# Adding the last expert sums apart from the stored rows, and a later first weight load, at a layer boundary

## The reference, cut to what matters

```python
# end of layer 0, for context and latent tokens alike
y = jnp.zeros_like(hf)
for e in range(N_EXPERTS):
    a = jax.nn.silu(hf @ w_gate[e]) * (hf @ w_up[e])
    y = y + combine[:, e:e + 1] * (a @ w_down[e])
x = x + g2 * y                        # ctx = ctx + cg2 * y
# start of layer 1
h = _rmsnorm(x, norm1[l]) * (1 + sc1) + sh1
q_a, k_a, v_a, q_b, k_b, v_b, q_n, k_n, v_n, gate_l = jnp.split(h @ w_in[l], IN_OFFSETS, axis=-1)
```

## Time and profile before

| | us |
|---|---|
| median of 3 runs | 1623.99 (1623.52 to 1628.21) |
| profiled execution, its own time | 1625.1 |
| profiled execution, span from first to last instruction | 1623.3 |
| TensorE busy | 1556.6 |
| granted clock, mean share of full | 0.975 |

### The profile page before, as it was taken

One profiled execution on the slowest core, in us unless ns is written; L12 is line 12 of the kernel. 1 busy time (PEld: TensorE's weight loads), 2 busy tenths in 40 slices (PEclk: granted clock), 3 DMA queues, 4 the chain that ended last, 5 costly groups with the idle time before them and its releaser, 6 DMA issues. The chain is left out here.

```text
span 1623.3 us, 16361 instructions
## 1 busy us (share of the span) xinstructions
PE 1556.6 (96%) x6186; PEld 743.0 (46%) x6186; DVE 658.9 (41%) x1409; ACT 340.1 (21%) x784; POOL 131.7 (8%) x212
## 2 busy tenths in 40 slices
PE   8999999999999999899999988999999998989796
PEld 4444456644444444654444434446654444433232
DVE  2232068776677724611111126503766327211113
ACT  3011178810000021101011014114830011100001
POOL 1000001200000010200100020000210010111010
PEclk9999999999999999899999998999999997999898
DMA  9912430135535360699999797543139775999996
GB/s 341 298 54 102 159 133 2 40 106 156 200 139 192 144 233 39 231 347 365 413 407 417 296 374 272 155 168 117 27 123 343 277 281 210 376 411 408 415 374 277
DMA packets 110528, 382.39 MB, mean 236 GB/s; under 512 B 24945, under 2 KB 29185, under 8 KB 93872
## 3 DMA queue, kind: packets, MB, share of 16 engines
q1 hardware_dynamic: 96112, 330.32, 54.6%
q0 software_dynamic: 13904, 50.71, 8.7%
q10 hardware_dynamic: 432, 0.29, 0.1%
HBM read 367.00 MB, written 30.47 MB: 245 GB/s over the span
## 5 line engine op out<-in xcount | busy, mean ns | idle before, releaser
L2180 PE MATMUL bank<-ring_sb,HT_sb 128*128 128x512 f32 x544 | 240.2, 594 | 0.0
L2077 PE MATMUL bank<-ring_sb,HT_sb 128*128 128x512 f32 x384 | 170.0, 598 | 2.5 <-ACT HT_sb L964 2.5
L2180 PEld LDWEIGHTS bank<-ring_sb,HT_sb 128*128 128x128 f32 x544 | 102.4, 190 | 131.8 <-issue 131.8
L1253 DVE SCALAR_TENSOR_TENSOR MB_sb<-ring_sb,cT_sb,MB_sb 128x512 f32<-128x512 f32 x192 | 144.3, 752 | 6.8
L2184 PE MATMUL bank<-ring_sb,QR_sb 128*128 128x512 f32 x288 | 129.5, 592 | 0.0
L2348 PE MATMUL bank<-ring_sb,HT_sb 128*64 128x512 f32 x544 | 123.4, 607 | 0.7 <-ACT HT_sb L1134 0.7
L2077 PEld LDWEIGHTS bank<-ring_sb,HT_sb 128*128 128x128 f32 x384 | 72.2, 192 | 89.3 <-issue 89.3
L2372 PE MATMUL bank<-ring_sb,QR_sb 128*64 128x512 f32 x336 | 82.4, 635 | 17.1 <-DMA ring_sb<-w_e_down 14.5
L2074 PE MATMUL bank<-HT_sb,ring_sb 128*128 128x512 f32 (+1 forms) x256 | 97.4, 539 | 0.0
L1097 ACT ACTIVATE WK_sb<-bank 128x512 f32<-128x512 f32 x36 | 21.5, 597 | 341.2 <-PE bank L2180 341.1
L2184 PEld LDWEIGHTS bank<-ring_sb,QR_sb 128*128 128x128 f32 x288 | 54.7, 190 | 68.9 <-issue 68.9
(11 more groups left out here) (356 smaller groups left out, 1759.0 us busy)
## 6 DMA issues: line engine op xcount, KB each, us to landing
ring_sb<-w_e_down SPq DMA_DIRECT2D x32, 2048.0 KB, 15.4
ring_sb<-w_mod SPq DMA_DIRECT2D x24, 2048.0 KB, 9.3
ring_sb<-w_in SPq DMA_DIRECT2D x21, 2048.0 KB, 17.7
ring_sb<-w_e_gate SPq DMA_DIRECT2D x16, 2048.0 KB, 12.0
ring_sb<-w_e_up SPq DMA_DIRECT2D x16, 2048.0 KB, 13.1
ring_sb<-w_e_gate SPq DMA_DIRECT2D x22, 1024.0 KB, 16.9
ring_sb<-w_e_up SPq DMA_DIRECT2D x22, 1024.0 KB, 18.6
ring_sb<-w_branch SPq DMA_DIRECT2D x8, 1024.0 KB, 12.8
```

The lines of the kernel that those rows point to most:

```text
L1253: link(stt(a, WR[slot][:, k], cT[:, k, strm:strm + 1], a, ALU.mult, ALU.add))
L2077: ins = mm(bank[j % 4][:, :], HT[:, k, P * t:P * t + P], WR[slot][:, k], start=(k == 0), stop=(k == KD - 1))
L2180: ins = mm(bank[i % 2][:, :], HT[:, k, P * t:P * t + P], WR[wg][:, k], start=(k == 0), stop=(k == KD - 1))
```

## The change

Three things. For tiles 0 and 1 first_rows no longer waits for TensorE's last sums and no longer adds them: it only multiplies the rows, over 1024 columns in one instruction, as it does for tiles 2 and 3. The last sums of tiles 0 and 1 are then gated and added by add_last, after add_rows. The scaling of tile 0 stands behind second_rows(1) in place of ahead of it. And SyncE awaits the gathered rows of tile 0 before it issues kvab of layer 1.

```diff
@@ SyncE, the loads of a layer
+                    if key == ("kvab", 1):
+                        eng.wait_ge(ygat_in[0], 32)
                     if key == ("qa", 1):
                         for t in range(NT):
                             eng.wait_ge(ygat_in[t], 32)
@@ VectorE, first_rows
                     y0 = ygat[t][0]
-                    if t < 2:
-                        eng.wait_ge(add_mm, NT * l + t + 1)
-                        for half in range(2):
-                            cols = slice(CW * half, CW * half + CW)
-                            ins = stt(y0[:, cols], y0[:, cols], r_w[:, t, 0:1], add_bank[t][half][:, :], ALU.mult, ALU.add)
-                        link(ins)
-                    else:
-                        link(ts(y0, y0, r_w[:, t, 0:1], None, ALU.mult))
+                    link(ts(y0, y0, r_w[:, t, 0:1], None, ALU.mult))
@@ VectorE, add_rows
                     link(tt(y0, y0, gout[:, t // NLAT], ALU.mult))
-                    ins = tt(X[:, t], X[:, t], y0, ALU.add)
-                    if t < 2:
-                        ins.then_inc(x_moe, 1)
-                        eng.wait_ge(x_moe, NT * l + t + 1)
-                    else:
-                        link(ins)
+                    link(tt(X[:, t], X[:, t], y0, ALU.add))
@@ VectorE, layer 0's end
                     for t in range(NT):
                         first_rows(t)
-                        if t:
+                        if t >= 2:
                             scaled(1, t - 1)
                         second_rows(t)
+                        if t == 1:
+                            scaled(1, 0)
                         add_rows(t)
-                        if t >= 2:
-                            add_last(t)
+                        add_last(t)
                     scaled(1, NT - 1)
```

## The result

| | us |
|---|---|
| kernel before, median of 10 runs beside it | 1625.76 (1622.90 to 1629.77) |
| changed kernel, median of 10 runs | 1630.20 (1626.47 to 1634.58) |
| ratio, 95% interval | 1.0029 (1.0016 to 1.0042) |
| span of the profiled execution | 1628.5 (before 1623.3) |

The change costs 4.7 us (2.6 to 6.8), where 1.5 was forecast, and 1630.2 lies above the range. In these runs the kernel before was itself 1.8 us above the median that the forecast started from, so 1.8 us of the miss is the base and some 3 us the change.

What follows compares the result with a forecast made beforehand. TensorE was taken to bound, the boundary's shift passing through: rows -1.2, order +2.13 and +0.48 give +1.4 us, topped to +1.5 by kvab's weights. Median 1623.99 becomes 1625.5; range 1622.8 to 1628.4.

Steps and rivals of the forecast that it cites:

- VectorE's order: Layer boundary: tile 0's last sums after its rows cost +2.13 us, its scaling behind second_rows(1) +0.48 us.
- what bounds, and that the boundary's shift is passed on: TensorE, busy 96% of the span, bounds; whatever the layer boundary gains or loses arrives at the end unchanged.
- Tile 0 starts at 967.85 - 1.2: Tile 0's first VectorE instruction: with kvab late, the gathered rows land 1.2 us sooner, at 966.65.
- (a): Store of yd ahead of the gathers: lands 0.6 us sooner without kvab's packets beside it, bounds 0 to 1.0.
- (b): Tile 0's gathers: land 0.6 us faster without kvab's last packets beside them, bounds 0 to 1.3.
- kvab goes out at about 966.75 ... I take the middle of these two, 980.6: kvab, issued among the gathers, lands at 980.6, between 980.1 and 981.1, 0.3 us ahead of VectorE's path.
- the upper bound: kvab's latest landing, 981.1: gathers' data from 962.3, 12.6 us for the gathers and 6.2 for kvab.
- the sum holds as long as kvab is the last to finish: Bus at the boundary: gathers' time plus kvab's gives kvab's landing, whatever share of packets each gets.
- The weights become the wait: Rival: kvab served only after the gathers, landing 984.1; TensorE +4.6, with the clock +5.3, whole time 1629.3; chance 0.12.

Runs made afterwards that it cites:

- e1: Changed kernel without SyncE's wait ahead of kvab, so only VectorE's new order, against the kernel before: ratio 1.0017 (1.0008 to 1.0026).
- e7: Kernel before with 20 unused products ahead of the last sums of tiles 0 and 1: ratio 1.0075 (1.0058 to 1.0092).
- e8: e1 with 20 unused products ahead of the last sums of tiles 0 and 1: ratio 1.0076 (1.0059 to 1.0093) against the kernel before.
- e2: Kernel before with only kvab's wait for tile 0's gathered rows added, VectorE's order unchanged: ratio 1.0018 (1.0008 to 1.0028).
- e3: Kernel before with kvab waiting for the gathered rows of all four tiles: one run, 1629.91 us, with 1626.11 for the kernel before beside it.
- e12: Kernel before with kvab waiting only for the stores of yd, as GpSimd does ahead of the gathers: ratio 1.0022 (1.0012 to 1.0033).
- e6: Kernel before with the down weights of layer 0's last expert as four DMAs with 4 KB packets instead of one with 16 KB: ratio 1.0007 (0.9991 to 1.0023).
- e4: Kernel before with only the second of kvab's two 1 MB pieces waiting for tile 0's rows: ratio 1.0000 (0.9989 to 1.0011).
- e11: e6 and e4 together, plus a separate semaphore for tile 0's first gather, against the kernel before: ratio 1.0002 (0.9991 to 1.0013).

## Why the prediction was wrong

**Right: VectorE's order.** Forecast +2.13 and +0.48 from tile 0's start to the scaled tile, +2.61; measured +2.60 in the changed kernel (10.62 to the transposes against 8.02) and +2.69 in e1. e7 and e8 show its reason: with the sums last, the same order gains 2.0 us.

**Right: what bounds, and that the boundary's shift is passed on.** wb0's load went out 4.3 to 5.5 us later, after the first product had come 4.4 to 5.0 later.

**Wrong: "Tile 0 starts at 967.85 - 1.2".** Half of this was to come from the store (a), half from the gathers (b). The store took 11.0 us in the changed kernel and 10.4 in e2, with kvab early 10.4, 11.1 and 10.6: nothing. From first gather to tile 0's start it took 7.05, 7.88 and, in e3, 6.94 us with kvab late, 6.94, 6.90 and 6.94 with it early: nothing. (The 7.88 is not kvab's doing either, which in e2 goes out only then; so a single profile can be off by 0.9 us here.) The early kvab lies in a gap: in the changed kernel, without it, the bus carried a single packet between 956 and 960, and before the change all but kvab's last packets had moved when the gathers' first came, at 962.8. Those last packets, until 964.2, do delay the first gather, which landed 5.1 us after its issue with kvab early and 4.2 or 4.3 in e2 and e3. But tile 0 waits for its second gather, and that took 5.6 in e3 as before. e12 shows what real contention would have been, 3.2 us, and no kernel but that one and e6 had it. The change removed a cost that was not there.

**Wrong, and the step that decided: "kvab goes out at about 966.75 ... I take the middle of these two, 980.6".** That is +14.6 from the last sums; it landed at +18.5. The sum had two terms: the gathers' data start, at -3.7, and from there 18.3 us until all that moves ahead of kvab's last packet has moved. The data started at -2.8, 0.8 us later, since the store gave the gathers nothing. The stretch was 21.3 us, 3.0 longer, and that is the term that was mis-sized. Its rate was right: forecast 6.3 MB in the 18.8 us of the upper bound, 0.335 MB/us; measured 7.0 MB from the gathers' first packet to kvab's last, in 20.7 us, 0.338. Its bytes were not. The prediction says that "the sum holds as long as kvab is the last to finish"; but it put qa's load behind kvab on the queue and left it out of the sum, and qa's packets did not wait for kvab's end. All packets of the changed kernel from 978 to 980.9:

```profile
DMA packets 757, 1.07 MB, mean 369 GB/s; under 512 B 15, under 2 KB 454, under 8 KB 757
```

The 303 that are not under 2 KB are qa's. Their 0.62 MB are 1.8 us at the measured rate; 0.6 us more passed from kvab's last packet to its landing, and 0.5 us is the choice of the middle over the upper bound. This split is worked out from the traces. e4 agrees with it, but no run holds qa back and leaves the rest, so what qa's packets cost is an estimate. What e3 does show is that a landing can't be had as issue time plus a duration here: issued 7.5 us later than in e2, kvab was there at the same moment.

So the first product started at the later of +16.8 (order, rows not sooner) and +18.5 (weights), not at +15. The rival *The weights become the wait* had given +4.6 at TensorE and 1629.3 for the whole; its wait was the case, and I gave it 0.12. That its number is close is in part luck: it had kvab moving only after the gathers and alone, and kvab in fact moved a third of its packets beside them and the rest mixed with qa's. The 14.7 us that kvab was early looked like slack to give away, and the later issue used all of it and 5 us more. The Trainium skill (DMA: Bandwidth & Descriptors, Rules for kernel authors) advises to issue a DMA early and wait late. The trace agrees with the advice; the page's reason is the fixed setup cost, and here it was the other traffic.

**Open.** In e2 the boundary lost 4.4 to 4.9 us and the whole time 2.9 (1.3 to 4.5); in e7 the boundary lost 15.4 to 16.1 and the whole time 12.2 (9.4 to 15.0). The profiles show no place that gives time back: from the first product to the end it took 643.8 and 643.4 us in the unchanged kernel, 644.9 in e2 and 644.1 in e7. But each is one execution, in e2 and e7 the slowest of those counted, and the second layer varied between them: the changed kernel took 665.5 us from the last sums to the end (1628.5 - 963.01), 8.2 more than the unchanged one (1623.3 - 965.97), of which the boundary explains 5. Of the other 3.2, 1.2 are TensorE's waits for w_e_down (15.7 against 14.5) and 1.7 one wait for VectorE (L2027 for KR_sb, 5.0 against 3.3), which in the other profiles that I compared lay between 3.2 and 4.7. Whether the second layer takes some of a shift back on average isn't settled.

## What to carry to other kernels

A load that goes out long before its use may be sitting in the only gap of the bus. Before it is moved behind something, ask what else is on the bus from its new issue to its use, and count all bytes that move before its last: those ahead of it, its own, and those of the loads queued behind it, which need not wait for its end. A share of the bus, or a time for the load by itself, gives too little. Splitting off the last part of an addition pays only if the part that is hidden is complete before the last operand arrives; read from the timeline which operand that is. And two costs that meet in one wait don't add: with the order undone (e2) the first product stayed at +18.5.

## What the runs showed of the hardware that I had not expected

TensorE's clock comes back at a moment that differs from run to run. After the standing at the boundary its granted clock is 0.50, 1.2 GHz, and it returns to 1.00 within the first tile's products. Stretches with busy times of PE, PEld, DVE, ACT, POOL, then PEclk, DMA share, GB/s, for e11 and for e4:

```profile
976.00:980.00 4.00, 2.57 (x3) 1.18 (x4) 2.08 (x3) 3.97 (x11) 0.00 (x0) 0.50 0.62 184
980.00:984.00 4.00, 4.00 (x10) 1.85 (x9) 3.75 (x5) 0.04 (x1) 0.00 (x0) 0.95 1.05 401
```

```profile
980.00:984.00 4.00, 4.00 (x6) 1.44 (x5) 2.65 (x4) 1.14 (x3) 0.00 (x0) 0.50 1.02 390
984.00:988.00 4.00, 4.00 (x12) 1.77 (x11) 1.91 (x2) 0.00 (x0) 0.00 (x0) 0.91 1.05 387
```

In e11 the first product starts at 977.43 and the clock is back at about 980.4, 3 us later; in e4 at 978.63 and 984.7, 6 us later. From the first product to the next tile's transposes this makes 7.6 to 9.1 us in the kernels here, a spread of 1.5 us that follows none of the edits, and more than half of what the order costs. The 3 us between the first two profiles are of this kind too: from 24 to 28 us the granted clock was 0.50 before the change and 1.00 in the changed kernel, in the same products.
